# Keeping the weights of expert pair 24 instead of pair 16 in SBUF, with octets 1 to 5 as one loop

## The reference

```python
aff = sigmoid(xt @ w_router)                    # 64 experts in 8 groups
eidx = top 8 experts of the 4 best groups       # for each of 256 tokens
gates = aff[eidx] / sum * 2.5
for each expert e, on the rows routed to it:    # D = 1024, hidden = 256
    h = silu(xb @ w_gate[e]) * (xb @ w_up[e])
    y = h @ w_down[e]                           # scattered back, times its gate
shared = (silu(xt @ ws_gate) * (xt @ ws_up)) @ ws_down
x = layer_norm(alpha * x + routed + shared)
```

## Time and profile before

| | us |
|---|---|
| median of 3 runs (1184.84 to 1185.89) | 1185.27 |
| the profiled execution | 1185.22 |
| its span in the trace | 1183.4 |
| TensorE busy with matmuls | 1148.8 (97%) |
| pair 0's gate products start at, layer 0 and layer 1 | 134.69, 732.21 |

### The profile page before, as it was taken

The page is one execution under the profiler, slowest core; times in us unless marked ns, Lnnn a source line. Parts: engine busy times, 40 slices in busy tenths (PEclk is TensorE's granted clock), DMA queues, the critical chain, the costliest instruction groups (busy, mean ns, idle before and its releaser), DMA issues.

```text
span 1183.4 us, 22172 instructions
## 1 busy us (share of the span) xinstructions
PE 1148.8 (97%) x8844; PEld 688.0 (58%) x8846; DVE 347.0 (29%) x912; ACT 299.6 (25%) x713; POOL 56.2 (5%) x100
## 2 busy tenths in 40 slices
PE   9999999999999999999999999999999899999995
PEld 6865755555555555554787647555555555555552
DVE  0445512222122212121523556222222222221224
ACT  1454222212122212122213523122221212221212
POOL 1431100000001000000011001000000010000000
PEclk9999999999999999999999999999999999999998
DMA  9965699999999999999991556999999999999995
GB/s 373 418 268 215 208 421 425 426 428 430 426 428 426 428 427 426 428 428 416 415 420 77 240 225 215 397 424 429 426 429 430 425 425 426 427 427 426 428 423 199
DMA packets 42444, 449.12 MB, mean 380 GB/s; under 512 B 4480, under 2 KB 4864, under 8 KB 14208
## 3 DMA queue, kind: packets, MB, share of 16 engines
q1 hardware_dynamic: 41360, 443.30, 89.9%
q10 hardware_dynamic: 1008, 4.73, 1.0%
HBM read 446.96 MB, written 1.05 MB: 379 GB/s over the span
## 4 chain that ended last, share of the span: by engine, by line
PE 85%; DMA 9%; DVE 3%; ACT 1%; issue 1%; DVEq 0%; SPq 0%; ACTq 0%
PE bank L1327 18%; PE bank L1354 17%; PE bank L1390 17%; PE bank L873 7%; PE bank L892 6%; PE bank L1398 5%; PE bank L935 4%; DMA ring<-in_w_gate 4%; DMA ring<-in_w_down 3%; DMA ring<-in_w_in_b 2%; PE bank L1363 2%; PE bank L1223 1%; PE bank L1094 1%; PE bank L1105 1%; ACT router_work L1524 1%
## 5 line engine op out<-in xcount | busy, mean ns | idle before, releaser
L1327 PE MATMUL bank<-ring,router_work 128*64 128x256 f32 x1984 | 227.8, 382 | 5.2 <-DMA ring<-in_w_gate 5.2
L1354 PE MATMUL bank<-ring,router_work 128*64 128x256 f32 x1952 | 225.2, 379 | 5.9 <-issue 5.9
L1390 PE MATMUL bank<-ring,router_work 128*32 128x512 f32 x1888 | 218.4, 595 | 3.2 <-ACT router_work L1524 3.0
L1327 PEld LDWEIGHTS bank<-ring,router_work 128*64 128x64 f32 x1984 | 137.0, 137 | 116.0 <-issue 41.9
L1354 PEld LDWEIGHTS bank<-ring,router_work 128*64 128x64 f32 x1952 | 144.8, 137 | 75.4 <-issue 10.8
L2057 DVE SCALAR_TENSOR_TENSOR yhalf<-bank,gcol,yhalf 128x512 fp32r<-128x512 f32 x124 | 93.0, 751 | 219.3 <-ACT yhalf L1691 219.3
L1691 ACT ACTIVATE yhalf<-bank,gcol 128x512 fp32r<-128x512 f32 x124 | 85.0, 687 | 172.3 <-PE bank L1390 172.3
L2049 DVE TENSOR_TENSOR router_work<-router_work,bank 128x256 f32<-128x256 f32 x64 | 27.0, 421 | 346.4 <-PE bank L1354 346.4
L1390 PEld LDWEIGHTS bank<-ring,router_work 128*32 128x32 f32 x1888 | 56.2, 109 | 122.4 <-issue 110.7
L1524 ACT ACTIVATE router_work<-bank 128x256 f32<-128x256 f32 (+4 forms) x229 | 92.0, 420 | 120.2 <-PE bank L873 47.3
L1524 ACT ACTIVATE back<-bank 128x128 fp32r<-128x128 bf16 x64 | 17.7, 277 | 281.5 <-PE bank L1297 281.5
(11 more groups left out here) (184 smaller groups left out, 847.8 us busy)
## 6 DMA issues: line engine op xcount, KB each, us to landing
ring<-in_w_gate SPq DMA_DIRECT2D x58, 2048.0 KB, 17.3
ring<-in_w_down SPq DMA_DIRECT2D x56, 2048.0 KB, 17.9
ring<-in_w_up SPq DMA_DIRECT2D x52, 2048.0 KB, 18.8
ring<-in_w_up SPq DMA_DIRECT2D x18, 1024.0 KB, 12.5
ring<-in_w_in_b SPq DMA_DIRECT2D x3, 3072.0 KB, 22.8
ring<-in_w_gate SPq DMA_DIRECT2D x8, 1024.0 KB, 7.7
ring<-in_w_down SPq DMA_DIRECT2D x6, 1024.0 KB, 10.3
out_first<-in_w_out SPq DMA_DIRECT2D x2, 2048.0 KB, 29.1
```

The costliest lines, as they stand in the source:

```text
L1327: last = pe.matmul(gate_bank[slots_of(e), 0:HID], xg[:, k, slots_of(2 * j + e)], w[e][:, k, :], start=(k == 0), stop=(k == KT - 1))
L1354: last = pe.matmul(up_bank[slots_of(e), 0:HID], xg[:, k, slots_of(2 * j + e)], w[e][:, k, :], start=(k == 0), stop=(k == KT - 1))
L1390: last = pe.matmul(yb[half][rows_of(t, e), :], hT[b][:, f, slots_of(e, t)], w[e][:, f, half * 512:half * 512 + 512], start=(f == 0), stop= ...
```

## The change

`RES_PAIR` goes from 16 to 24, the first pair of octet 6, which is the octet of the shared products. The constants of the SP queue follow (`RES_STEP` from 8 to 12: the first SP loop goes from five turns to nine, the second from five to one), as do the index of the matrices that `keep` loads and the counts that POOL and `load_norm` wait for. On TensorE, octets 1 to 5 are one loop of five turns, and octet 6 is written out with both the kept pair and the shared products.

```diff
-RES_PAIR = 16
+RES_PAIR = 24
 RES_STEP = RES_PAIR // UNROLL
-RES_OCTET = RES_PAIR // OCT_PAIRS
 SHARED_OCTET = OCTETS - 2
+assert RES_PAIR == SHARED_OCTET * OCT_PAIRS
...
                     for j in range(OCT_PAIRS):
                         unit(r, 0, j, place=j)
-                    with pe.Fori(1, RES_OCTET) as o:
+                    with pe.Fori(1, SHARED_OCTET) as o:
                         for j in range(OCT_PAIRS):
                             unit(r, o, j)
                     for j in range(OCT_PAIRS):
-                        unit(r, RES_OCTET, j, kept=(j == 0), kept_before=(j == 1))
-                    with pe.Fori(RES_OCTET + 1, SHARED_OCTET) as o:
-                        for j in range(OCT_PAIRS):
-                            unit(r, o, j)
-                    for j in range(OCT_PAIRS):
-                        unit(r, SHARED_OCTET, j, shared=j)
+                        unit(r, SHARED_OCTET, j, kept=(j == 0), kept_before=(j == 1), shared=j)
                     for j in range(OCT_PAIRS):
                         unit(r, OCTETS - 1, j, last=(j == OCT_PAIRS - 1))
```

## The result

| | before | with the change |
|---|---|---|
| median, us | 1185.89 (5 runs, 1184.84 to 1187.15) | 1203.64 (5 runs, 1202.92 to 1205.31) |
| span in the trace | 1183.4 | 1201.1 |

The ratio is 1.0152, with a 95% interval of 1.0137 to 1.0167: slower, by 17.8 us, against +18.55 forecast.

What follows compares the result with a forecast made beforehand. TensorE (13.31 us a pair) was taken as bound until its lead over full-queue weight transfers (14.70 us a pair) runs out. 10.99 + 11.02 - 1.27 - 1.18 - 1.01 = +18.55 us gave 1203.8 us, range 1201.5 to 1208.

Steps and rivals of the forecast that it cites:

- Pairs 16 to 23 at the transfers' pace: Eight MoE pairs per layer now each take a transfer's 14.70 us: +10.99 us in layer 0, +11.02 in layer 1.
- What is given back: Waits that vanish behind kept pair 24: -1.27 us in layer 0, -1.18 in layer 1, -1.01 between layers.
- the ends: Pairs 30 and 31 of each layer no longer wait for weights: -1.27 us in layer 0, -1.18 in layer 1.
- the seam: From layer 0's last downs to layer 1's first loads: the query projection's whole wait comes back, -1.01 us.
- Code at nothing: One octet fewer written out, one loop more turned on TensorE, and SP's queue work: priced at 0.
- The lead: Transfers' margin ahead of TensorE in each MoE: 1.39 us used per pair, 14.70 gained at the kept pair.
- A: Rival: lead behind pair 24 is lost, pairs 30, 31 and the seam wait as before; +22.0, 1207.2 us; chance 0.05.
- B: Rival: TensorE's clock falls in the stretch with waits; 190 us on top at half clock, or 1224 us; chance 0.01.
- C: Rival: transfers keep up in pairs 16 to 23, needing 472 GB/s, so faster: 1181.8 us; chance 0.02.
- D: Rival: the change doesn't do what it says, bytes and order of loads stay the same: 1185 us; chance 0.01.
- POOL's 4.78 us in the shared octet: POOL rebuilds `x` behind the kept pair, beside pair 18 before, in the shared octet now: priced at 0.

Runs made afterwards that it cites:

- e7: The changed kernel with the three loads of pair 16 left out in both layers, its products reading old ring contents: 1181.82 us.
- e6: The kernel of e1 with five matmuls of zeros added behind the gate products in each pair of octets 4 and 5: 1205.97 us.
- e2: The kernel before with the kept pair moved from 16 to 20, shared products staying in octet 6: 1192.18 us.
- e1: The kernel before with kept pair 24 but TensorE's octets written as before (1 to 3 looped, 4 written out, 5 a one-turn loop): 1206.12 us.
- e9: The changed kernel, unchanged, timed again on the chip of the later code-layout runs: 1204.06 us.
- e11: The changed kernel with octets 1 and 2 written out and octets 3 to 5 a loop: 1205.97 us.
- e5: The kernel before (kept pair 16) with five matmuls of zeros behind the gate products in each pair of octets 4 and 5: 1202.85 us.

## Why the prediction was right

**Pairs 16 to 23 at the transfers' pace.** Forecast 8 x 14.70 = 117.60 us from up to up. Measured 452.73 - 335.27 = 117.46 in layer 0 and 1058.55 - 941.05 = 117.50 in layer 1, that is +10.85 and +10.92 where I had +10.99 and +11.02. e7 shows that the transfers are the cause, e6 that TensorE has this time to spare, e2 that half of the pairs costs about a third (6.2 of 17.8 us), since what is given back is the same for both.

**What is given back.** Right in kind, too small in size. I had taken the idle times in brackets: 1.27 and 1.18 us at the ends, 1.01 at the seam. Measured by starts, octet 7 is 1.60 and 1.66 us shorter, and the seam 1.29 (164.95 to 163.66). The reason is in the earlier trace rows: gate to up is 319.98 - 315.03 = 4.95 us there and 441.27 - 437.77 = 3.50 without a wait, 1.45 more, while the bracket says 1.27. The bracket begins where the last matmul is modelled to end, and without a wait the next ones overlap it. Each wait costs some 0.18 us more than its bracket. The sum of the three is 4.55 instead of 3.46.

**Code at nothing.** This step failed, to the good side: I priced the loop that replaces written-out octets at 0 because TensorE shows no gap at loop ends. It has none, but code comes through the DMA engines that are the bound, and the changed kernel has 42 packets of q8 where the kernel before has 57. e1, with the new place and the old code, is 2.5 us slower than the changed kernel (2.1 against e9); 2.2 us of this lie in its octets 4 and 5. So the place alone costs some 20.1 us, 1.6 more than my sum, and the loop takes some 2 us off. That both together came within 0.8 us of the forecast is in part luck. (By e1's interval the place costs 18.5 to 22.5 us, so my sum is at its edge.) Whether before would gain by fewer packets too, no run shows.

The terms come to 10.85 + 10.92 - 4.55 = 17.2; the span moved by 17.7. The rest is scatter of three points that I had taken as fixed. The lead ends elsewhere: octets 2 and 3 together take 111.3 us in layer 0 before and 112.6 after, 112.1 and 111.5 in layer 1. Layer 0's first gate starts 0.71 us earlier (133.98 after 134.69). What follows the last down products of layer 1 takes some 0.3 us more.

**The rivals.** A fell: no waits behind pair 24 in either layer. B fell: clock 1.00 in all stretches with waits. C fell: 428 GB/s in these stretches. D fell with the `home` gate at 465.84. POOL's 4.78 us in the shared octet cost nothing: octet 6 takes 60.5 us before and after.

## What to carry to other kernels

Where two pipelined resources have nearly the same pace, a saving on the slower one is worth what the faster one still has time to spend behind it: a skipped transfer placed too late leaves its lead unspent at the end (the queue idle there), one placed too early overfills the buffers (idle behind it), and between these the place doesn't matter (pairs 12 and 16 here, the same to 0.1%). Work out the lead along the whole stage, its peaks at the ends of octets included, from the starts of operations rather than from the idle times beside them.

## What the runs showed of the hardware

Instructions come through the DMA engines that carry the weights (q8, 57 packets and 0.93 MB before, 42 and 0.69 MB after). With the queue full at 428 GB/s, 15 packets of code more (0.24 MB) went with 1.9 to 2.5 us more, whether they came in the stretch in which TensorE waits (e1) or mostly ahead of it (e11); 0.24 MB at that rate would be 0.6 us. Why it is several times that stays open, and so does whether the packets alone are the cause.

In e5's octets 4 and 5 a matmul of 512 columns of bf16 zeros is listed at 0.38 us, and five in a row at 1.25 us, while they lengthened the pair by 1.35.
